# Gate rows by way of memory instead of products of a diagonal with ones

## The chip, the core and the metric

The kernel runs as one program on one core of a Trainium2 chip. The metric is the device time of one execution in microseconds (us). Three executions of the kernel before took 3296.44, 3298.0 and 3299.87 us, median 3298.0.

## The reference

256 tokens of width 2048 pass two blocks, all in float32. The first block is a feed-forward layer, an attention layer and a second feed-forward layer, closed by a norm. The second block has two layers. In each of them, with `c_act = silu(c)` for the token stream and `cc_act = silu(c_ctx)` for a context stream of another 256 tokens:

```python
shift, scale, gate = jnp.split(c_act @ w_mod + b_mod, 3, axis=-1)
shift_c, scale_c, gate_c = jnp.split(cc_act @ w_mod + b_mod, 3, axis=-1)
h = rms_norm(x, norm_g) * (1 + scale) + shift          # the same with _c for the context
p = h @ w_in
x_new = x + gate * mix_out(p, ...)                     # mix_out ends in  @ w_out
xc    = xc + gate_c * mix_out(pc, ...)                 # only in the first of the two layers
```

`gate` and `gate_c` are one row of 2048 numbers each, the same for all tokens. The change is about how this row comes to stand on all 128 partitions, where the residual's sum needs it.

## The kernel before, in words

Tokens lie on partitions in tiles of 128, features on the free axis. The first layer of the second block works on four such tiles (two of tokens, two of context, `nt` = 4), the second layer on two. Every weight matrix is streamed once from memory in units of 512 KB into a ring of four (`raw`), each unit holding two pieces of 128 rows by 512 columns. ScalarE rounds a piece to `hi` (L421), VectorE makes the rest `lo` (L425), and TensorE multiplies each token tile three times per piece: L430 and L431 with `hi`, L435 with `lo`. `hi` and `lo` are rings of four pieces. A piece so takes 6 products with two tiles and 12 with four.

SyncE issues the weight loads (L572), each as soon as the slot's last piece has been made into `lo`. The matrix of the modulation (`wmt`, which gives shift, scale and gate) comes between them: its products are sums on VectorE (L1240, L1242) during the two feed-forward layers of the first block. GpSimd's queue carries other loads: half of `wmt`, small tables, pieces of the norm's gain (`ogc`, L2554) and the context (`cst`, L2564), and writes of x to memory (`x_rest`, L2598, L2614).

The gate lies after `modulation` as `mG[p, layer, stream, k]`, with feature `128 k + p` on partition p (L1192). The out-projection of a layer (`phase o2`) needs it as `gatb[any partition, stream, feature]`. Its 2048 output columns come in four chunks `c` of 512, each with 16 pieces `j`; after chunk c, `add_gated(c, t)` on VectorE multiplies the accumulated tile t by `gatb` (L1887) and adds x (L1892). The gate rows for it are made in strips of 512, eight in the first layer, four in the second, at pieces named in `gate_at`: VectorE lays the gate's numbers on the diagonals of four 128 x 128 blocks (`dg`, L1902), TensorE multiplies a matrix of ones by them (L2520), which puts every number on all partitions, and ScalarE copies the result out of PSUM (L1117).

Each engine runs its own instruction list in order; the places in them are written out by hand as (chunk, piece) positions. `gatb` lies over the last quarter of `qkvg`, which is read for the out-projection's inputs up to the twelfth of its 16 row groups (`o_hi`, `o_low`, L1874).

Of the kernel before, what the change touches and what calls it, by code (L numbers as in the profile page):

```python
# [17 lines left out]
F32 = mybir.dt.float32  # L18
F32R = mybir.dt.float32r
ACT = mybir.ActivationFunctionType  # L20
ALU = mybir.AluOpType
# [77 lines left out]
        self.pieces, self.taken, self.groups, self.fulls, self.turns = pieces, taken, groups, fulls, turns  # L99


def build(nc, a, out, xs_dram):
    ctx = ExitStack()
    with ctx:
        sem_names = """raw0 raw1 raw2 raw3 hi_made lo_made pieces_used acc_done acc_taken tp_done tg_full tg_hi
# [2 lines left out]
            o_done o_taken lam_e ob_made x4_in xs_out ctx_in c_raw c_again modg0 modg1 modd0 modd1 mod_done silu_c  # L108
            ca_const_in glu_made gates_made yt_done yt_taken pl_done pl_taken py_done py_taken pad_made
            conv_step cf_in cf_done z_made cz_done s_made pw_done yc_made na_in bias_in nil_made rot_made  # L110
            st_dve pt_done pt_taken gs_done gs_taken x4r_in fin_in y_out gate_diag rs_made cf_sd zt_done zt_taken w_made og_in s_diag sbc_done mods_made y1_made sig_made ag_made gc_made hq_made tq_done tq_taken
            tmp_made y_made gr_made gt_done gt_taken""".split()
        S = {n: ctx.enter_context(nc.semaphore(n)) for n in sem_names}
        base = (nc.sbuf_base + 63) // 64 * 64
# [59 lines left out]
        cv = at("cv", Q + 73 * K1, [P, 4, 2 * L])  # L174
        ya = at("ya", Q + 83 * K1, [P, 4, CH])
        gC = at("gC", Q + 91 * K1, [P, 4, CH])
        dg = at("dg", Q + 83 * K1, [P, 2, CH])


        Tq = [at("Tq0", H + 4 * K1, [P, CH]), at("Tq1", H, [P, CH])]  # L180
# [161 lines left out]
        def wait(eng, name, value):  # L342

            if not isinstance(value, int) or value > 0:
                eng.wait_ge(S[name], value)
# [8 lines left out]
        def kt_of(n):  # L354

            u, half = spot(n)
            return 2 * u + half

        def gate_at(nt, c, j):

            at_ = ((0, 8), (0, 9), (1, 3), (1, 4), (1, 7), (1, 8), (2, 3), (2, 4)) if nt == 4 else \
                ((0, 8), (1, 3), (2, 3), (3, 3))
            return [at_.index((c, j))] if (c, j) in at_ else []

        def strip_of(nt, i):

            return (i % 2, i // 2) if nt == 4 else (0, i)

        def o_bank(nt, k):

# [294 lines left out]
        def _(act):  # L665
# [330 lines left out]
            for ly in range(2):  # L996
# [114 lines left out]
                def o2_side(c, j, ly=ly, nt=nt):  # L1111
                    if c == 0 and j < 16:
                        o_hi(j)
                    for i in gate_at(nt, c, j - 6):
                        who, k = strip_of(nt, i)
                        act.wait_ge(S["gs_done"], 8 * ly + i + 1)
                        act.activation(gatb[:, who, k * CH:(k + 1) * CH], cg[i % 2][:], ACT.Copy).then_inc(S["gs_taken"], 1)  # L1117
                    if c == 0:
                        return
                    for t in range(nt):  # L1120
                        if j == 5 + 2 * (t // 2) + t % 2:
                            act.wait_ge(S["acc_taken"], phases[f"o2{ly}"].taken + nt * (c - 1) + t + 1)
                            square(sqj2[:, t % 2], x4[:, t, (c - 1) * CH:c * CH], ssp[:, t, c - 1:c])
                    if ly == 0 and j == 10:
                        z_take(zst2, 1, 0, c - 1)
                    if ly == 0 and j == 12:
                        z_take(zst2, 1, 1, c - 1)
                    if c == 3 and j == 14:

                        act.activation(zs[:, 5:6], ones[:, 0:1], ACT.Sqrt)  # L1130
                    if ly == 0 and c == 3 and j == 15:
                        last_sums(ly, nt)
                        z_take(zst2, 1, 0, 3)
# [19 lines left out]
        def _(dve):  # L1153
# [524 lines left out]
            for ly in range(2):  # L1678
# [200 lines left out]
                def add_gated(i, t, ly=ly, nt=nt):  # L1879
                    cols = bass.ds(i * CH, CH)  # L1880
                    if t == 0:
                        if i == 0:
                            dve.wait_ge(S["x4r_in"], 32 if ly == 0 else 48)
                        dve.wait_ge(S["gs_taken"], 8 * ly + nt // 2 * (i + 1))

                    dve.wait_ge(S["acc_taken"], phases[f"o2{ly}"].taken + t - 1 + nt * i)
                    dve.tensor_tensor(tm2[:, t % 2], acc[first_bank(nt, i) + t][:], gatb[:, t // 2, cols], ALU.mult)\  # L1887
                       .then_inc(S["tmp_made"], 1)
                    v = (16 if ly else 0) + t + 1 + nt * i
                    dve.wait_ge(S["tmp_made"], v)  # L1890
                    xv = x4[:, t, cols]
                    dve.tensor_tensor(xv, tm2[:, t % 2], xv, ALU.add).then_inc(S["acc_taken"], 1)  # L1892
                def o2_side(c, j, ly=ly, nt=nt):
                    if c == 0 and j < 16:
                        o_low(j)
                    for i in gate_at(nt, c, j):
                        who, k = strip_of(nt, i)
                        wait(dve, "gs_done", 8 * ly + i - 1)
                        if i == 0:

                            dve.wait_ge(S["tp_done"], phases[f"mx{ly}"].turns + 4)
                        dve.tensor_tensor(dg[:, i % 2].rearrange("p (k n) -> p k n", n=P),  # L1902
                                          ident[:].unsqueeze(1).broadcast_to([P, 4, P]),
                                          mG[:, ly, who, 4 * k:4 * k + 4].unsqueeze(2).broadcast_to([P, 4, P]),
                                          ALU.mult).then_inc(S["gate_diag"], 1)
                    if ly == 0:
                        if c == 0 and j in (6, 9):
                            modulation(1, (6, 9).index(j))
                        if c == 3 and j == 15:
                            for t in range(2):  # L1910
                                bank_done(dve, phases["o20"], 4, 3, t)
                                add_gated(3, t)
                            z_sums(0, 2, 14)
                            dve.tensor_scalar(zv[:, 0:2], zv[:, 0:2], 1.0 / D, EPS, ALU.mult, ALU.add)\
                               .then_inc(S["var_made"], 1)
                            z_reciprocal(0, 2)
                            z_diag(0, 2)
                            bank_done(dve, phases["o20"], 4, 3, 2)
                            add_gated(3, 2)
                    elif c and j in (9, 10):  # L1920
                        dve.wait_ge(S["fin_in"], 16)
                        w_tile(x4, fgain[:, (c - 1) * CH:c * CH], j - 9, c - 1)
# [25 lines left out]
        def _(pe):  # L1948
# [366 lines left out]
            for ly in range(2):  # L2315
# [198 lines left out]
                def o2_side(c, j, ly=ly, nt=nt, ring=ring, o_turn=o_turn):  # L2514
                    if c == 0 and j + ring in O_TURNED:
                        o_turn(j + ring)
                    for i in gate_at(nt, c, j - 1):
                        pe.wait_ge(S["gate_diag"], 8 * ly + i + 1)
                        wait(pe, "gs_taken", 8 * ly + i - 1)
                        pe.matmul(cg[i % 2][:], ones[:], dg[:, i % 2], start=True, stop=True).then_inc(S["gs_done"], 1)  # L2520
                    if ly == 0 and c and j in (8, 10):
                        t0 = j - 8
                        pe.wait_ge(S["acc_taken"], phases["o20"].taken + 4 * (c - 1) + t0 + 2)
                        z_turn(x4, t0, (c - 1) * CH)
# [16 lines left out]
                                 (lambda j, ly=ly: pe.wait_ge(S["tg_lo"], phases[f"mx{ly}"].groups + j + 1))  # L2541
                                 if c == 0 else None, c == 3, x_ready if c == 3 else None)
                if ly == 0:
                    pe.wait_ge(S["gs_taken"], 8)
                    rows_over(2, 0, 2)
                    fill(cg[1], 4)

# [2 lines left out]
        def _(pool):  # L2550
# [38 lines left out]
            for c in range(1, 4):  # L2589
                ctx_load(c)  # L2590
                gain_load(c)
            for ly in range(2):
                nt = NT[ly]

                if ly == 0:
                    for t in range(2):
                        pool.wait_ge(S["x4_in"], t + 1)
                        pool.dma_start(xs_v[:, t], x4[:, t, :]).then_inc(S["xs_out"], 16)  # L2598

                if ly == 1:  # L2600
                    pool.wait_ge(S["conv_step"], 132)

                    pool.wait_ge(S["tg_full"], phases["n41"].fulls + 16 + 6)
                pool.memset(yT[:, :, :, 0:PAD], 0.0).then_inc(S["pad_made"], 1)
                pool.memset(yT[:, :, :, PAD + L:YW], 0.0).then_inc(S["pad_made"], 1)


                pool.wait_ge(S["cf_in"], 32 * (ly + 1))
                pool.memset(nil, 0.0).then_inc(S["nil_made"], 1)
                if ly == 0:  # L2610
                    for c in range(4):

                        pool.wait_ge(S["acc_taken"], phases["o20"].taken + 4 * c + 2)
                        pool.dma_start(xs_v[:, :, c * CH:(c + 1) * CH], x4[:, 0:2, c * CH:(c + 1) * CH])\  # L2614
                            .then_inc(S["xs_out"], 16)
            pool.wait_ge(S["tg_lo"], phases["o21"].groups)
            pool.dma_start(fgain[:], row_bc(a["final_norm_g_2"], D)).then_inc(S["fin_in"], 16)

# [25 lines left out]
```

## Time and profile before

| | us |
|---|---|
| median of three executions | 3298.0 |
| lowest, highest | 3296.44, 3299.87 |
| span of the profiled execution (first to last instruction) | 3296.4 |
| TensorE busy in it | 3250.2 |
| VectorE busy | 2271.8 |
| ScalarE busy | 1554.2 |
| GpSimd busy | 90.8 |

The profile gives the profiled execution's own time as this span alone; the three times are of other executions, and their median lies 1.6 us above it. "Busy" counts overlapping instructions once. A matmul's duration in the profile is the time from its start to its modelled end; since matmuls are pipelined, what one costs is the distance between starts.

### The profile page before, as it was taken

Reading aid. Unit: us, or ns where it says so; the run is one execution under the profiler, and the core shown is the slowest. Engines: PE = TensorE matmul, PEld = TensorE weight load, DVE = VectorE, ACT = ScalarE, POOL = GpSimd, SP = SyncE. Lnnn points to the kernel's source line nnn. Section 1 sums busy time; section 2 is a strip of 40 time slices with the busy share of each in tenths; the row PEclk is TensorE's granted clock in tenths of the full one; section 3 lists DMA queues with packets and bytes.
Section 4 is the critical chain, followed back from the end, with each engine's and each line's share of the span. In section 5 each row is a group of like instructions: output and inputs, shape, how many; then the busy total and the mean of one; then the engine's idle time right before and its main releaser. Section 6 shows DMA issues by size and latency. Waiting matters only on the chain.

```text
span 3296.4 us, 40653 instructions
## 1 busy us (share of the span) xinstructions
PE 3250.2 (99%) x15142; PEld 2650.1 (80%) x15142; DVE 2271.8 (69%) x4132; ACT 1554.2 (47%) x2872; POOL 90.8 (3%) x174
## 2 busy tenths in 40 slices
PE   9999999999999999999999999999999999999998
PEld 7888888888888788888888788888866778888766
DVE  7888888877776788888877633557556437746666
ACT  6545454445665555445555422222256336522464
POOL 0000000000000000000000000000000000000000
PEclk9999999999999999999999999999999999999999
DMA  8888877776545888788877432333322236533525
GB/s 285 261 267 262 258 260 259 251 260 197 153 147 173 260 260 268 260 259 260 268 261 264 131 104 89 95 100 96 96 80 78 86 100 192 181 116 96 176 72 171
DMA packets 285316, 614.21 MB, mean 186 GB/s; under 512 B 18688, under 2 KB 21312, under 8 KB 283456
## 3 DMA queue, kind: packets, MB, share of 16 engines
q1 hardware_dynamic: 261792, 527.50, 50.0%
q0 software_dynamic: 21952, 80.69, 7.5%
q10 hardware_dynamic: 1376, 3.44, 0.3%
q8 instruction: 120, 1.97, 0.2%
q14 instruction: 76, 0.62, 0.1%
HBM read 605.26 MB, written 6.29 MB: 186 GB/s over the span
## 4 chain that ended last, share of the span: by engine, by line
PE 93%; ACT 2%; DVE 2%; DMA 1%; issue 1%; SPq 0%; ACTq 0%; DVEq 0%
PE acc L430 29%; PE acc L431 28%; PE acc L435 28%; PE tp L2434 1%; PE acc L2455 1%; PE acc L2420 1%; DMA raw<-ffn_w_gu 1%; PE tp L2393 1%; PE tp L2002 1%; ACT pr L1068 0%; PE cgw L2405 0%; DVE lo L425 0%; PE cgw L2155 0%; PE tp L1964 0%; ACT hi L421 0%
## 5 line engine op out<-in xcount | busy, mean ns | idle before, releaser
L421 ACT ACTIVATE hi<-raw 128x512 fp32r<-128x512 f32 x1808 | 1135.1, 632 | 1546.7 <-PE acc L435 1472.5
L425 DVE TENSOR_TENSOR lo<-raw,hi 128x512 fp32r<-128x512 f32 x1808 | 1208.3, 689 | 832.4 <-ACT hi L421 823.3
L430 PE MATMUL acc<-hi,hT_hi 128*128 128x512 f32 x1760 | 696.2, 396 | 9.3 <-DVE hT_lo L1227 4.9
L431 PE MATMUL acc<-hi,hT_lo 128*128 128x512 f32 x1760 | 685.4, 389 | 0.0
L430 PE MATMUL acc<-hi,h_hi 128*128 128x512 f32 x1696 | 670.9, 396 | 6.8 <-ACT hi L421 3.8
L431 PE MATMUL acc<-hi,h_lo 128*128 128x512 f32 x1696 | 662.0, 390 | 0.0
L435 PE MATMUL acc<-lo,h_hi 128*128 128x512 f32 x1696 | 533.9, 390 | 0.4 <-DVE lo L425 0.4
L435 PE MATMUL acc<-lo,hT_hi 128*128 128x512 f32 x1760 | 513.6, 389 | 0.0
L430 PEld LDWEIGHTS acc<-hi,hT_hi 128*128 128x128 f32 x1760 | 330.4, 188 | 87.9 <-DVE hT_lo L1227 8.9
L431 PEld LDWEIGHTS acc<-hi,hT_lo 128*128 128x128 f32 x1760 | 330.6, 188 | 69.1 <-issue 2.6
L435 PEld LDWEIGHTS acc<-lo,hT_hi 128*128 128x128 f32 x1760 | 330.5, 188 | 69.1
L430 PEld LDWEIGHTS acc<-hi,h_hi 128*128 128x128 f32 x1696 | 319.1, 188 | 74.4 <-ACT hi L421 5.5
L435 PEld LDWEIGHTS acc<-lo,h_hi 128*128 128x128 f32 x1696 | 319.2, 188 | 68.6 <-DVE lo L425 0.8
L431 PEld LDWEIGHTS acc<-hi,h_lo 128*128 128x128 f32 x1696 | 319.4, 188 | 64.5
L430 PE MATMUL acc<-hi,uT_hi 128*128 128x512 f32 x704 | 275.3, 391 | 0.5 <-DVE lo L425 0.5
L431 PE MATMUL acc<-hi,uT_lo 128*128 128x512 f32 x704 | 274.0, 389 | 0.0
L1240 DVE CUSTOM_DVE_ANT_0 cgw<-mw,cb 128x1024 f32<-128x1024 f32 x192 | 235.6, 1227 | 0.7 <-DMA mw<-wmt 0.7
L1242 DVE CUSTOM_DVE_ANT_0 mw<-mw,cb 128x1024 f32<-128x1024 f32 x192 | 234.5, 1221 | 0.0
L435 PE MATMUL acc<-lo,uT_hi 128*128 128x512 f32 x704 | 219.9, 389 | 0.0
L1742 DVE SCALAR_TENSOR_TENSOR cv<-yT,dw,cv 128x512 f32<-128x512 f32 (+1 forms) x256 | 156.7, 612 | 0.0
L430 PEld LDWEIGHTS acc<-hi,uT_hi 128*128 128x128 f32 x704 | 132.2, 188 | 28.3 <-DVE lo L425 1.4
L435 PEld LDWEIGHTS acc<-lo,uT_hi 128*128 128x128 f32 x704 | 132.2, 188 | 27.7
(283 smaller groups left out, 2155.9 us busy)
## 6 DMA issues: line engine op xcount, KB each, us to landing
raw<-ffn_w_gu SPq DMA_DIRECT2D x352, 512.0 KB, 5.8
raw<-w_in SPq DMA_DIRECT2D x280, 512.0 KB, 3.8
raw<-ffn_w_down SPq DMA_DIRECT2D x176, 512.0 KB, 5.4
mw<-wmt POOLq DMA_DIRECT2D x132, 512.0 KB, 5.6
raw<-w_out SPq DMA_DIRECT2D x96, 512.0 KB, 4.1
mw<-wmt SPq DMA_DIRECT2D x60, 512.0 KB, 5.9
ball<-rpbx SPq DMA_DIRECT2D x8, 768.0 KB, 9.8
x<-x_rest SPq DMA_DIRECT2D x2, 2048.0 KB, 7.8
```

What stands on the lines that cost most here:

```text
L421: act.activation(hi[:, g % RING, :], raw_piece(g), ACT.Copy).then_inc(S["hi_made"], 1)
L425: dve.tensor_tensor(lo[:, g % RING, :], raw_piece(g), hi[:, g % RING, :].bitcast(F32), ALU.subtract).then_inc(S["lo_made"], 1)
L430: pe.matmul(bank, act_hi, hi[:, slot, :], start=start, stop=False)
L431: pe.matmul(bank, act_lo, hi[:, slot, :], start=False, stop=False)
L435: return pe.matmul(bank, act_hi, lo[:, slot, :], start=False, stop=stop)
L1240: dve.tensor_tensor_reduce(cgw[:].rearrange("p a n -> p (a n)"), w, c[:, 0], 1.0, 0.0, ALU.mult, ALU.add, dst[:, 0:1])
L1242: dve.tensor_tensor_reduce(w, w, c[:, 1], 1.0, 0.0, ALU.mult, ALU.add, dst[:, 1:2])\
L1742: dve.scalar_tensor_tensor(out=av, in0=yv, scalar=dw[:, ly, bass.ds(j * 16 + s, 1)], in1=av, op0=ALU.mult, op1=ALU.add).then_inc(S["conv_s ...
L2002: ins = pe.transpose(tp[f][:, k * L + t * P:k * L + (t + 1) * P], ub[:, t, (2 * f + k) * P:(2 * f + k + 1) * P], ident[:])
L2393: ins = pe.matmul(tp[t % 2][:], sT[:, t % 2, c * P:(c + 1) * P], cpw[:, c, :], start=(c == 0), stop=(c == 3))
L2420: ins = pe.matmul(acc[e][:], q[r, t * P:(t + 1) * P], kk[r, :], start=True, stop=True)
L2434: ins = pe.transpose(tp[u % 2][:, j * P:(j + 1) * P], src, ident[:])
```

## The change

The twelve strips made with diagonals, products with ones and copies go away, with their buffer and semaphores. Instead GpSimd's queue writes both gate rows of a layer to a small buffer in memory (`gate_rows`, 2 layers x 2 streams x 2048), and in the out-projection reads each chunk's 512 columns back with a partition step of zero, so that all 128 partitions get the same row. The write of the first layer stands behind the loads of `ogc` and `cst`, that of the second behind the writes of `x_rest` in the first layer's out-projection. The reads stand in each layer behind the `memset` of `nil`, and wait for the write and for the twelfth row group. `add_gated` waits for its chunk's read.

```diff
-def build(nc, a, out, xs_dram):
+def build(nc, a, out, xs_dram, gate_rows):
-        dg = at("dg", Q + 83 * K1, [P, 2, CH])
@@ ScalarE, out-projection
-                    for i in gate_at(nt, c, j - 6):
-                        who, k = strip_of(nt, i)
-                        act.wait_ge(S["gs_done"], 8 * ly + i + 1)
-                        act.activation(gatb[:, who, k * CH:(k + 1) * CH], cg[i % 2][:], ACT.Copy).then_inc(S["gs_taken"], 1)
@@ VectorE, add_gated
-                        dve.wait_ge(S["gs_taken"], 8 * ly + nt // 2 * (i + 1))
+                        dve.wait_ge(S[f"gat_in{i}"], 16 * (ly + 1))
@@ VectorE, out-projection
-                    for i in gate_at(nt, c, j):
-                        who, k = strip_of(nt, i)
-                        wait(dve, "gs_done", 8 * ly + i - 1)
-                        if i == 0:
-                            dve.wait_ge(S["tp_done"], phases[f"mx{ly}"].turns + 4)
-                        dve.tensor_tensor(dg[:, i % 2]..., ident..., mG[:, ly, who, 4 * k:4 * k + 4]..., ALU.mult)
@@ TensorE, out-projection
-                    for i in gate_at(nt, c, j - 1):
-                        pe.wait_ge(S["gate_diag"], 8 * ly + i + 1)
-                        wait(pe, "gs_taken", 8 * ly + i - 1)
-                        pe.matmul(cg[i % 2][:], ones[:], dg[:, i % 2], start=True, stop=True).then_inc(S["gs_done"], 1)
...
-                    pe.wait_ge(S["gs_taken"], 8)
@@ GpSimd
+            def gates_out(ly):
+                pool.wait_ge(S["mods_made"], 2 * ly + 2)
+                pool.dma_start(gate_rows[ly].rearrange("w (k p) -> p w k", p=P), mG[:, ly], allow_slow_non_contiguous=True).then_inc(S["gm_out"], 16)
+
+            gates_out(0)
             for ly in range(2):
...
                 pool.memset(nil, 0.0).then_inc(S["nil_made"], 1)
+                pool.wait_ge(S["gm_out"], 16 * (ly + 1))
+                pool.wait_ge(S["tg_lo"], phases[f"mx{ly}"].groups + 12)
+                for c in range(4):
+                    rows = bass.AP(tensor=gate_rows.tensor, offset=gate_rows[ly, 0, c * CH:(c + 1) * CH].offset,
+                                   ap=[[0, P], [D, nt // 2], [1, CH]])
+                    pool.dma_start(gatb[:, 0:nt // 2, c * CH:(c + 1) * CH], rows).then_inc(S[f"gat_in{c}"], 16)
                 if ly == 0:
...
+                    gates_out(1)
```

## Rows read from the trace of the kernel before

**Rows 1.** The page's first part: engine, busy us, share, instructions.

```profile
PE 3250.2 (99%) x15142; PEld 2650.1 (80%) x15142; DVE 2271.8 (69%) x4132; ACT 1554.2 (47%) x2872; POOL 90.8 (3%) x174
```

**Rows 2.** The chain that ended last, shares, 2530 to 2745 us.

```profile
by line: PE acc L430 27.7%; PE acc L431 26.8%; PE acc L435 26.8%; PE cgw L2520 3.2%; DVE tm L1887 2.9%; PE tp L1964 2.6%; issue 2.5%; PE tp L2508 1.5%; DVE x L1892 1.1%; PE acc L2455 0.8%; PE cgw L1952 0.8%; ACT hi L421 0.7%; ACT zst L727 0
```

**Rows 3.** The same chain, shares, 3180 us to the end.

```profile
by line: PE acc L430 24.4%; PE acc L431 23.9%; PE acc L435 23.9%; PE cgw L2520 2.9%; PE acc L2455 2.6%; PE acc L2420 1.9%; PE tp L2434 1.8%; ACT x L1146 1.7%; ACT pr L1063 1.3%; issue 1.2%; ACT hi L421 1.0%; PE tp L2508 0.7%; ACT L1130 0.6%
```

**Rows 4.** Timeline of TensorE: start us, us, engine, line, what.

```profile
2559.88 1.07 PE L435 MATMUL acc<-lo,hT_hi 128*128 128x512 f32 x4
2562.60 1.07 PE L435 MATMUL acc<-lo,hT_hi 128*128 128x512 f32 x4
2563.51 1.02 PE L2520 MATMUL cgw<-dg,ones 128*128 128x512 f32 x2
2566.19 1.07 PE L435 MATMUL acc<-lo,hT_hi 128*128 128x512 f32 x4
```

**Rows 5.** By tile: duration ns min/median/max, first and last start us.

```profile
L2520 PE MATMUL cgw<-dg,ones x24: 590/591/595, 2563.5 to 3268.7; 128*128 128x512 f32 x24
...
L1902 DVE TENSOR_TENSOR dg<-ident,mG x12: 683/686/692, 2552.0 to 3264.9; 128x512 f32<-128x512 f32 x12
...
L1117 ACT ACTIVATE gatb<-cgw x12: 579/580/622, 2575.5 to 3271.3; 128x512 f32<-128x512 f32 x12
```

**Rows 6.** The page's groups: busy us, mean ns, idle before.

```profile
L421 ACT ACTIVATE hi<-raw 128x512 fp32r<-128x512 f32 x1808 | 1135.1, 632 | 1546.7 <-PE acc L435 1472.5
L425 DVE TENSOR_TENSOR lo<-raw,hi 128x512 fp32r<-128x512 f32 x1808 | 1208.3, 689 | 832.4 <-ACT hi L421 823.3
```

**Rows 7.** Timeline of GpSimd around the two new writes.

```profile
1771.83 0.58 POOL L2554 DMA_DIRECT2D ogc<-out_norm  x1 [34.10 <-DVE x L1583]
1843.86 0.56 POOL L2598 DMA_DIRECT2D x_rest<-x  x1 [71.45 <-ACT x L976]
...
2726.90 0.72 POOL L2614 DMA_DIRECT2D x_rest<-x  x1 [42.18 <-DVE x L1892]
```

**Rows 8.** DMA queues, 744 to 762 us: packets, MB, share of 16 engines.

```profile
q1 hardware_dynamic: 1434, 2.78, 46.7%
q0 software_dynamic: 464, 0.98, 34.0%
```

**Rows 9.** DMA queues, 750 to 755 us.

```profile
q0 software_dynamic: 254, 0.48, 75.8%
q1 hardware_dynamic: 226, 0.42, 22.9%
```

**Rows 10.** Landing of weight loads (L572) issued in 744 to 764, then 1740 to 1810 us.

```profile
DMA to landing us min/median/max: 3.7/5.1/10.2
...
DMA to landing us min/median/max: 3.9/5.4/9.1
```

**Rows 11.** Waits of ScalarE: us, times, longest; 740 to 775, then 1770 to 1790 us.

```profile
ACT hi L421 <- DMA raw<-w_in: 2.6, 1, 2.6
...
ACT hi L421 <- DMA raw<-ffn_w_down: 1.9, 1, 1.9
```

**Rows 12.** Windows: us, busy PE, PEld, DVE, ACT, POOL; PEclk, DMA share, GB/s.

```profile
1760.00:1780.00 20.00, 20.00 (x90) 16.57 (x89) 16.38 (x28) 11.94 (x23) 0.58 (x1) 1.00 0.76 243
...
2724.00:2734.00 10.00, 9.96 (x49) 8.13 (x48) 6.46 (x14) 5.57 (x14) 0.72 (x1) 1.00 0.22 82
...
3210.00:3215.00 5.00, 5.00 (x25) 4.11 (x24) 3.12 (x6) 2.69 (x6) 0.55 (x1) 1.00 0.59 170
```

**Rows 13.** Timeline of VectorE: twelfth row group in each layer, first use in the second.

```profile
2559.54 0.68 DVE L1874 TENSOR_TENSOR hT_lo<-qkvg,hT_hi 128x512 fp32r<-128x512 f32 x1
...
3205.81 0.42 DVE L1874 TENSOR_TENSOR hT_lo<-qkvg,hT_hi 128x256 fp32r<-128x256 f32 x1
...
3215.74 0.69 DVE L1887 TENSOR_TENSOR tm<-acc,gatb 128x512 f32<-128x512 f32 x1 [0.62 <-PE acc L435]
```

**Rows 14.** First layer's uses of the gate rows, first and last start.

```profile
L1887 DVE TENSOR_TENSOR tm<-acc,gatb x15: 682/684/692, 2581.7 to 2728.6; 128x512 f32<-128x512 f32 x15
```

**Rows 15.** DMA issues: size of each, median us from issue to landing.

```profile
ogc<-out_norm POOLq DMA_DIRECT2D x4, 256.0 KB, 5.9
psc<-pool_scale SPq DMA_DIRECT2D x2, 256.0 KB, 7.7
```

More of the change, by code:

```diff
@@ L110, in build @@
             conv_step cf_in cf_done z_made cz_done s_made pw_done yc_made na_in bias_in nil_made rot_made
-            st_dve pt_done pt_taken gs_done gs_taken x4r_in fin_in y_out gate_diag rs_made cf_sd zt_done zt_taken w_made og_in s_diag sbc_done mods_made y1_made sig_made ag_made gc_made hq_made tq_done tq_taken
+            st_dve pt_done pt_taken gm_out gat_in0 gat_in1 gat_in2 gat_in3 x4r_in fin_in y_out rs_made cf_sd zt_done zt_taken w_made og_in s_diag sbc_done mods_made y1_made sig_made ag_made gc_made hq_made tq_done tq_taken
             tmp_made y_made gr_made gt_done gt_taken""".split()
@@ L357, in kt_of @@
             return 2 * u + half
[L359 to L367, printed above, removed]
         def o_bank(nt, k):
@@ L1895, in o2_side @@
                         o_low(j)
-                    for i in gate_at(nt, c, j):
-                        who, k = strip_of(nt, i)
-                        wait(dve, "gs_done", 8 * ly + i - 1)
-                        if i == 0:
-                            dve.wait_ge(S["tp_done"], phases[f"mx{ly}"].turns + 4)
[L1902 to L1905, printed above, removed]
                     if ly == 0:
@@ L2640 @@
     xs = nc.dram_tensor("x_rest", (L, D), F32, kind="Internal").ap()
-    build(nc, aps, out, xs)
+    gates = nc.dram_tensor("gate_rows", (2, 2, D), F32, kind="Internal").ap()
+    build(nc, aps, out, xs, gates)
     r = run_bass_kernel_spmd(nc, [arrays], core_ids=[0])
```

## The prediction

> **What bounds the kernel now.** I read the page's busy shares first: TensorE is busy 3250.2 of 3296.4 us [rows 1], so a microsecond that TensorE need not spend is worth nearly a microsecond wherever nothing else ends later. Then the chain of waits of the two stretches in which the gate rows are made and used: of the first layer's out-projection (2530 to 2745 us) 3.2% is L2520, the products with ones [rows 2]; of the stretch from 3180 us to the end it is 2.9% [rows 3]. The diagonals (L1902) and the copies (L1117) don't appear in either list. So TensorE's part of the old way is on the path and the other two parts are beside it. Third, because the change puts new transfers on GpSimd's queue, the timeline of that queue, the share of the DMA engines in windows, and how late weights land.
>
> **What goes from TensorE.** The timeline shows the price of one strip: L435 starts at 2559.88, 2562.60 and 2566.19 [rows 4]. A piece without a strip takes 2.72 us, the one with it 3.59, so a strip costs 0.87 us. Each is recorded as two passes of 591 ns, 24 records for 12 strips [rows 5]; their distance counts, not their sum. 12 x 0.87 is 10.4 us. The chain gives the same by another way: 3.2% of 215 us is 6.9, 2.9% of 116.4 us is 3.4, together 10.3 [rows 2, 3]. I take 10.3.
>
> **What goes from VectorE and ScalarE.** 12 x 0.686 = 8.2 us and 12 x 0.580 = 7.0 us [rows 5]. Both lie beside TensorE's products; ScalarE spends most of its idle time waiting for TensorE [rows 6]. I put 0 for them. If TensorE then met something later, it would be VectorE's row groups in the first chunk, and these get earlier too.
>
> **The new write of gate rows, first layer.** It is issued right behind the load of `ogc`, at 1772.4 us; GpSimd's next instruction in the old order comes at 1843.86 [rows 7], so 71 us of delay in the queue would hide. The issue itself took 0.56 to 0.72 us in neighbouring DMAs [rows 7]. Its result is needed some 790 us later. What it can cost is the weights: by the change's own access pattern a partition's neighbouring numbers lie 512 bytes apart in memory, so this is 2 x 16 x 128 = 4096 pieces of 4 bytes, 256 for each DMA engine, while the last feed-forward projection streams its weights.
>
> The trace has nothing of 4 bytes. The nearest are GpSimd's 13 small loads of tables at 744 to 752 us: from the tile shapes, 2176 rows of 128 to 1024 bytes, with 13 x 16 = 208 completions 2384 items. They took 34.0% of 16 engines over 18 us, 97.9 us of engine time for 0.98 MB; the weights beside them took 134.5 us for 2.78 MB, 48.4 us per MB [rows 8]. So an item cost 41 ns in all, or 21 ns when the bytes are taken out at the weights' rate. A far upper end is the densest window's 60.6 us for 254 packets, 239 ns, if each 4-byte piece cost as much as such a packet [rows 9]. For one engine's 257 items (256 and a completion) that is 5.4, 10.5 or 61 us. I take 31 ns, between the two lower values, since the pieces carry no bytes to speak of but go to memory: 8.0 us.
>
> While they drain, the weights' queue is pushed back: in the densest window it had 22.9% of the engines beside 75.8% for GpSimd's [rows 9], where the stretch at 1760 to 1780 us uses 0.76 [rows 12]. Weights are then late by 1 - 0.229/0.76 = 0.70 of the drain: 3.8, 5.6, 7.4 or 43 us.
>
> How much lateness is free? A weight load in this stretch lands 5.4 us after its issue in the median, 9.1 at the most, and ScalarE waited 1.9 us for one [rows 10, 11]. Taking these as the same load, `hi` is wanted 7.2 us after the issue. With four `hi` pieces in the ring and 1.36 us per piece (half of 2.72, two tiles instead of four), a `hi` that starts on time stands three pieces, 4.1 us, before TensorE needs it, less 0.63 and 0.69 us for making `hi` and `lo` [rows 6]: 2.8 us more. So 10.0 us from issue to TensorE, of which 5.4 are used: 4.6 us are free. The small loads at 744 us agree: a load landed at 10.2 instead of 5.1 us, ScalarE waited 2.6 us [rows 10, 11]. The stall is 5.6 - 4.6 = 1.0 us; at 21 ns 0, at 41 ns 2.8, at 239 ns 38.
>
> The Trainium skill says in "DMA: Bandwidth & Descriptors", section "Rules for kernel authors", that a non-contiguous last dimension becomes one descriptor per element, and in its "Queues, rings and completion order" that an engine changes between queues only at packet boundaries, a packet holding up to 64 descriptors. The trace agrees that small descriptors push the weights back (22.9% [rows 9]); by the rule with 64 pieces to a packet the weights would get even less than I assume, and complete exclusion at 41 ns would make the stall 10.5 - 4.6 = 5.9 us instead of 2.8. No row here shows packets of 4-byte pieces.
>
> **The write of the second layer** comes behind the last `x_rest` at 2726.90 [rows 7]. There the engines are used to 0.22 [rows 12] and with four tiles a piece lasts 2.72 us, so twice the lateness is free. 0 us; with the 61 us drain it would reach into the next layer and cost some 10.
>
> **The reads back.** First layer: GpSimd waits until the twelfth row group, 2559.54 + 0.68 = 2560.2 us, then issues four reads of 512 KB. The first use is at 2581.7 [rows 13, 14], 21 us later, or some 20 when two strips are gone. Second layer: released at 3206.2, first use at 3215.74 [rows 13], less one strip 3214.9: 8.7 us for a broadcast of 256 KB. The same kind of load from the same queue (`ogc`) landed in 5.9 us, `psc`, which stood behind others, in 7.7 [rows 15]. Both fit, by 2.8 and 1.0 us. The later chunks have 21 us and more. The 1 MB read there fits beside weights that use 0.59 of the engines [rows 12]; 0 us, up to 2 if a weight unit is held back. Behind the new wait in `add_gated` stand the `lo` pieces of the next chunk on VectorE, and TensorE waits for them; behind GpSimd's new waits stand only the `x_rest` writes of the first layer, wanted after the first chunk, and `fgain`, wanted 20 us later.
>
> **The sum.** -10.3 + 1.0 = -9.3 us. Against the profiled span, 3296.4 to 3287.1; the median stands 1.6 us above that span, so 3288.7, rounded 3289.
>
> **The rivals.**
> 1. The 4-byte write eats most of the gain: its items cost 48 to 81 ns, the stall is 0.70 x 257 x price - 4.6 = 4 to 10 us. For it: writes to memory in pieces this small are outside all rows; against it: 21 to 41 ns in rows 8. At 60 ns: stall 6.2, time 3294.
> 2. Slower: the same write starves the weights for good. Break-even is a stall of 10.3, at 83 ns; measurably slower from 119 ns. At 150 ns the drain is 38.6 us, late by 27, stall 22.4: 3310. For it: the 239 ns packet in rows 9; against it: that packet carried 1.9 KB.
> 3. The reads in the second layer come late: at 12 us instead of 5.9 VectorE waits 3.3 us, its slack of under 1 us is gone, and TensorE loses about 3: 3292. For it: only 1.0 us of cover by `psc`.
> 4. TensorE's freed time is refilled by a wait: 3298. Against it: L1902 and L1117 are on neither chain [rows 2, 3].
>
> **How the numbers follow.** What a measurement of this kernel can tell from no change is about 0.2%, 6.6 us. Forecast 0.55 (all of it faster by over 6.6), rival 1 0.21, rival 3 0.05 and rival 4 0.03 (all within), rival 2 0.16 (slower). So 0.55, 0.29, 0.16. The likeliest case's own range is 3287.7 (no stall) to 3290.5 (2.8 us of it) and 1 us around it for the medians. The range for all reaches through rival 1 and into rival 2: 3286 to 3302.
>
> **What would show it.** Right: no L2520, L1902, L1117; pieces of 2.72 us throughout the out-projection; GpSimd with two small DMAs near 1772 and 2727 us and eight reads; DMA share near 1.0 for some 8 us after 1772 and at most one wait of `hi` for weights there with under 2 us of TensorE idle; VectorE's first L1887 in each layer still released by TensorE. Wrong: a wait of TensorE of over 4 us between 1772 and 1830 us, `tm` waiting for the gate read, or the landing of the small write beyond 20 us.

## Result and the profile after

The changed kernel takes 3304.45 us (median of 13 executions, 3299.67 to 3308.91) beside 3298.15 us for the kernel before (13 executions, 3296.32 to 3300.53): ratio 1.0019, 95% interval 1.0011 to 1.0026. It is slower by some 6 us, where 9 us less was forecast, and the time lies outside the range that was given (3286 to 3302 us). The profiled execution took 3306.85 us with a span of 3305.0.

The page's first part shows that the products are gone: 24 TensorE instructions fewer than in [rows 1], 12 fewer each on VectorE and ScalarE, ten more on GpSimd.

```profile
PE 3245.9 (98%) x15118; PEld 2648.1 (80%) x15118; DVE 2264.0 (69%) x4120; ACT 1547.6 (47%) x2860; POOL 99.2 (3%) x184
```

TensorE's busy time fell by only 4.3 us though 10.3 us of products left, and the span grew by 8.6. GpSimd's timeline tells where time came in. It is to be laid beside [rows 7]:

```profile
1772.25 0.58 POOL L2524 DMA_DIRECT2D ogc<-out_norm  x1 [34.10 <-DVE x L1568]
1772.82 1.70 POOL L2565 DMA_DIRECT2D gate_rows<-mG  x1
1859.59 0.57 POOL L2574 DMA_DIRECT2D x_rest<-x  x1 [85.06 <-ACT x L965]
...
2734.05 0.72 POOL L2596 DMA_DIRECT2D x_rest<-x  x1 [42.21 <-DVE x L1877]
2734.76 1.71 POOL L2565 DMA_DIRECT2D gate_rows<-mG  x1
2799.03 0.21 POOL L2580 MEMSET yT<- 128x120 f32 x1 [62.56 <-DVE tm L1204]
```

Up to the first new write the two kernels run within 0.5 us of each other. The next landmark stood at 1843.86 us and stands at 1859.59: 15.7 us lost, or 15.3 when both are counted from the `ogc` load just before the write. The last `x_rest` write of the first layer's out-projection stood at 2726.90 and stands at 2734.05, so by then 8.6 us have been won back; the eight strips of this layer explain 7.0 of it (8 x 0.87). The next landmark, the filling of `yT`, was at 2788.02 us in the profile before and is at 2799.03: 11.0 us late, so 3.9 us were lost behind the second write. The four strips of the second layer bring the difference to 8.6 us at the end.

The chain of waits names the carrier at both places; columns are start, us, what:

```profile
1778.18 23.30 DMA raw<-ffn_w_down
...
2741.93 12.36 DMA raw<-w_in
```

A weight load issued at 1778.18 us, 5.4 us behind the small write, took 23.3 us instead of the 5.4 of [rows 10]. The one before it, issued at 1776.84 us, took 20.9. TensorE's waits around the first and the second write (columns as in [rows 11]):

```profile
PE acc L419 <- ACT hi L410: 10.7, 2, 9.9
...
PE acc L419 <- ACT hi L410: 2.7, 1, 2.7
```

And the windows over the first, columns as in [rows 12]; the first line is of the kernel before, the others of the change:

```profile
1778.00:1790.00 12.00, 12.00 (x59) 10.03 (x58) 7.70 (x13) 7.45 (x17) 0.00 (x0) 1.00 0.83 267
...
1778.00:1790.00 12.00, 10.53 (x51) 8.48 (x49) 5.12 (x9) 3.99 (x8) 0.00 (x0) 1.00 1.13 64
1790.00:1798.00 8.00, 0.00 (x0) 0.00 (x0) 0.00 (x0) 0.21 (x1) 0.00 (x0) 0.56 0.92 114
1798.00:1808.00 10.00, 8.75 (x20) 6.39 (x21) 6.17 (x10) 4.76 (x11) 0.00 (x0) 0.50 0.74 274
```

Two things are to be seen. The DMA engines are recorded as fully busy while they move 64 GB/s, where the same stretch before moved 267. (The view adds up the times of packets, which overlap, so the share can pass 1.) And after TensorE has stood idle, it works at half its clock: the granted clock is 0.50, that is 1.2 instead of 2.4 GHz, from about 1791 to 1808 us, and TensorE works in it from 1798.5 on. The starts of its products lie 0.43 us apart there instead of 0.23. So the loss of 15.3 to 15.7 us is 10.7 us of waiting and some 4.5 us of slow products after it.

The queues from 1783 to 1793 us, columns as in [rows 8]:

```profile
q1 hardware_dynamic: 299, 0.68, 98.4%
q0 software_dynamic: 19, 0.00, 5.4%
```

The small write hardly shows as a user of the engines. It is the weights' own packets that got long: 98.4% of 16 engines over 10 us for 299 packets, 527 ns each. In the kernel before the same 10 us held 1335 packets of this queue with 82.7%, 99 ns each.

The reads back did what was expected. Landing of the four reads of the first layer and of the second, and VectorE's first use in the second layer:

```profile
DMA to landing us min/median/max: 7.8/9.6/10.1
...
DMA to landing us min/median/max: 6.0/6.7/7.7
...
3226.57 0.69 DVE L1872 TENSOR_TENSOR tm<-acc,gatb 128x512 f32<-128x512 f32 x1 [0.62 <-PE acc L424]
```

The second layer's reads were issued from 3218.2 us and landed within 7.7 us, before 3226.57, and the use still waited for TensorE, not for the read. The cover was 0.7 us (8.4 us from issue to use).

### The profile page after: what moved, and what is told of

It reads as the page before. It is cut to its first block, busy times and chain, and to the rows that moved or that the text cites. A ratio compares the mean times of both kernels' runs of the same rounds, so it can differ in the third digit from the quotient of the medians.

```text
span 3305.0 us, 40581 instructions
## 1 busy us (share of the span) xinstructions
PE 3245.9 (98%) x15118; PEld 2648.1 (80%) x15118; DVE 2264.0 (69%) x4120; ACT 1547.6 (47%) x2860; POOL 99.2 (3%) x184
## 4 chain that ended last, share of the span: by engine, by line
PE 93%; ACT 2%; DVE 2%; DMA 2%; issue 1%; SPq 0%; ACTq 0%; DVEq 0%
PE acc L419 29%; PE acc L420 28%; PE acc L424 28%; PE tp L2409 1%; PE acc L2430 1%; PE acc L2395 1%; DMA raw<-ffn_w_down 1%; PE tp L2368 1%; PE tp L1977 1%; DMA raw<-ffn_w_gu 1%; ACT pr L1057 0%; PE cgw L2380 0%; DVE lo L414 0%; PE cgw L2130 0%; DMA raw<-w_in 0%
## 5 line engine op out<-in xcount | busy, mean ns | idle before, releaser
L419 PE MATMUL acc<-hi,uT_hi 128*128 128x512 f32 x704 | 277.3, 394 | 11.2 <-ACT hi L410 10.7
```

Source lines behind the costliest of these rows:

```text
L419: pe.matmul(bank, act_hi, hi[:, slot, :], start=start, stop=False)
```

## Experiments

Theory after the trace: the whole loss comes from the writes of the gate rows, 4096 pieces of 4 bytes each, which hold up weight loads; the rest of the change is worth its 10.3 us of gain. Rivals: the reads or the new waits cost too; the cost is fixed per DMA; it comes from GpSimd's descriptor making; it comes from the number of pieces at the DMA engines; it comes from writing 4 bytes to memory. All ratios are against the kernel before on the same chip. In every kernel below `second_late`, and in `second_late` itself, the second layer's write goes in the attention stage as in `late`; where the first place has only a copy (`contig`, `onchip`, `spread`, `own_rows`), the first layer's real write goes there too.

| kernel | median us | ratio | 95% interval | against `late`, us | first write in the trace, us |
|---|---|---|---|---|---|
| the change | 3304.45 | 1.0019 | 1.0011 to 1.0026 | +16 | +15.3 |
| late | 3288.79 | 0.9970 | 0.9958 to 0.9981 | | +0.1 |
| writes_only | 3317.29 | 1.0055 | 1.0042 to 1.0069 | | +9.8 |
| second_late | 3299.12 | 1.0001 | 0.9992 to 1.0010 | +10 | +9.2 |
| half | 3295.14 | 0.9986 | 0.9977 to 0.9996 | +5 | +5.6 |
| contig | 3288.96 | 0.9969 | 0.9957 to 0.9981 | 0 | +0.1 |
| onchip | 3289.34 | 0.9963 | 0.9952 to 0.9975 | -2 | 0.0 |
| actq | 3301.12 | 1.0007 | 0.9998 to 1.0017 | +12 | +11.3 |
| paced | 3316.16 | 1.0054 | 1.0036 to 1.0071 | +28 | +29.0 |
| parted | 3296.39 | 0.9992 | 0.9982 to 1.0002 | +7 | +7.2 |
| spread | 3293.91 | 0.9980 | 0.9971 to 0.9990 | +3 | +5.2 |
| own_rows | 3306.48 | 1.0023 | 1.0014 to 1.0032 | +17 | +18.4 |

The fifth column is the difference of the ratios times 3298. Both ratios have their intervals, and `late` was measured on one chip only, so this column is good to some 5 us. The last column is taken within one execution: the distance from the `ogc` load to the next `x_rest` write [rows 7], less the 72.0 us that it has in the kernel before. Where nothing is lost it repeats within 0.2 us (before, `late`, `contig`, `onchip`). The three traces with the same whole write from GpSimd's queue (the change, `writes_only`, `second_late`) differ by 6 us among themselves.

**late**: both writes at a quiet time.

```diff
-            gates_out(0)
...
                 pool.memset(nil, 0.0).then_inc(S["nil_made"], 1)
+                pool.wait_ge(S["bias_in"], 64 * (ly + 1))
+                gates_out(ly)
                 pool.wait_ge(S["gm_out"], 16 * (ly + 1))
...
-                    gates_out(1)
```

> Both writes of the gate rows moved to each layer's attention, after the bias has landed, when the DMA engines are nearly idle. Theory (the whole loss is the two writes colliding with the weight loads at 1772 and 2735 us): the 10.3 us of the products remain, 3298.2 - 10.3 = 3287.9, within 2 us; no wait of ScalarE for weights over 3 us anywhere, clock 0.997. Rival (the reads back, or the new waits, cost as well): 3291 or more. Rival (the products' time is refilled): 3296 or more.

Measured 3288.79 us, as the theory had it. Its other sign did not hold as stated: ScalarE still has a wait of 5.0 us for weights, in the first block; the kernel before has one of 4.8 there. The write sits at 2430.8 and 3122.4 us, 130 and 79 us ahead of the reads. The stretch from 1770 to 1810 runs at full clock. TensorE's timeline at the place of the first strip, to be read beside [rows 4]:

```profile
2562.78 1.07 PE L424 MATMUL acc<-lo,hT_hi 128*128 128x512 f32 x4
2565.50 1.07 PE L424 MATMUL acc<-lo,hT_hi 128*128 128x512 f32 x4
```

2.72 us between them where the strip had made it 3.59. This version beats both kernels, by 10 and 16 us. What the reads, the waits and the order of the change cost is too small to be measured (the interval of `late` is 4 us to either side).

**writes_only**: the kernel before, and only the two `gates_out` added at the change's places, with a wait for them before the load of `fgain`.

> The kernel before with the two writes of the gate rows added at the places of the change; the rows are not read, the strips are made as before. Theory: plus 15 to 20 us (profile of the change: 15.8 at the first write, 3.9 at the second), 3313 to 3318. Rival (the collision needs something else of the change): under 3305.

3317.29 us, 18 us above the kernel before. So the writes need nothing else of the change to do their harm, and -10.3 + 18.4 gives the change's result to 2 us.

**second_late**: the first write where the change has it, the second moved as in `late`.

> The first write where the change has it, the second in the second layer's attention. Theory: the second write costs 3.9 us, so 3304.5 - 3.9 = about 3300.5. Rival (the second write only moves a wait that other work would have hidden): 3304.

3299.12 us: of the 16 us that lie between the change and `late`, the first write makes 10 and the second about 6 by the ratios. The trace of the change had 15.7 and 3.9 in one execution; the single executions of such kernels scatter (3296.44 to 3304.63 here). The one in this trace was the shortest: TensorE waited 6.4 us for `hi`, and the first write cost 9.2.

**half**: at the first place only stream 0, 2048 pieces; stream 1 goes in the attention stage. `gates_part(ly, w, k0, k1)` writes columns `k0` to `k1` of stream `w`.

```diff
-            gates_out(0)
...
+            gates_part(0, 0, 0, KT)
```

> At the first place only the token stream's row is written, 2048 pieces instead of 4096; the context's row and the second layer's rows go in the attention stages. Theory by pieces (lateness of a weight load grows with their number, 17.9 us for 4096, and 4.6 us are free): lateness 9, stall 4.4 us, TensorE's clock does not fall, 3287.9 + 4.4 = 3292. Rival (a fixed cost per such write): about 3300, like with the whole one. Rival (threshold): 3288.

3295.14 us, +5 where +4.4 was expected and +10 is the whole write; in its trace +5.6. So about half the pieces, half the cost: no threshold that 2048 stay under, and no fixed cost of the size of the whole. The intervals alone would not tell `half` from `late`, but `late` has no wait of TensorE for `hi` at this place and `half` has one of 3.8 us. That TensorE's clock would not fall was wrong: the granted clock of 1780 to 1790 us was 0.83. The proportion is then partly chance, since the free slack should have taken more of the half than of the whole.

**contig**: the same 16 KB as 128 rows of 128 bytes at the first place.

```diff
+            pool.wait_ge(S["mods_made"], 2)
+            pool.dma_start(gate_copy[:], mG[:, 0].rearrange("p w k -> p (w k)")).then_inc(S["gm_out"], 16)
```

> At the first place the same 16 KB go to memory as 128 rows of 128 bytes (a copy nobody reads); the rows that are read are written in the attention stages as in the run late. Theory (the number of 4-byte pieces makes the delay): no stall, 3289, like late. Rival (any write from GpSimd's queue there delays the weights): over 3293.

3288.96 us, nothing lost. A write to memory at that place is free when it is 128 pieces of 128 bytes.

**onchip**: 4096 pieces of 4 bytes, 8 bytes apart in each partition, but into a tile on chip whose contents nobody needs then.

```diff
+            pool.wait_ge(S["mods_made"], 2)
+            for w in range(2):
+                pool.dma_start(qss[:].rearrange("p a b -> p (a b)")[:, 0:2 * KT].rearrange("p (k w) -> p w k", w=2)[:, :, w],
+                               mG[:, 0, w], allow_slow_non_contiguous=True).then_inc(S["gm_out"], 16)
```

> At the first place 4096 pieces of 4 bytes go, in two DMAs of 2048, from the gate's tile to another tile on chip (nobody reads it) instead of to memory; the rows that are read are written in the attention stages. Theory A (the engines' work per piece delays the weights): 3299, like second_late. Theory B (4-byte writes to memory are what is slow): 3289, like late.

3289.34 us, nothing lost: theory B. As many pieces, the same queue, and no harm. GpSimd's issue of each DMA took 1.16 us, as long as the issue of 2048 pieces in `half` (1.17), so as much was made of it. Its DMAs of 2048 pieces landed in 7.9 and 8.3 us, where the 2048 of `half`, to memory and beside the same weights, took 14.5. The number of pieces alone does not hold up the weights; that they go to memory does. The Trainium skill says in "DMA: Bandwidth & Descriptors", section "Why small descriptors are slow (HBM only)", that transfers within SBUF don't suffer the penalty of small descriptors; the run agrees (+0 on chip, +10 to memory).

**actq**: the first write at the same time from ScalarE's hardware queue.

```diff
+                if c == 3 and j == 13:
+                    act.wait_ge(S["mods_made"], 2)
+                    act.dma_start(gate_rows[0].rearrange("w (k p) -> p w k", p=P), mG[:, 0],
+                                  allow_slow_non_contiguous=True).then_inc(S["gm_act"], 16)
```

> The first write at the same time and of the same 4096 pieces, but issued by ScalarE into its hardware queue; the second write in the attention stage. If the delay comes from GpSimd's making of descriptors: 3289, like late. If it comes from the pieces at the DMA engines or in memory: about 3299, like second_late, or more if the issue holds ScalarE up.

3301.12 us, +12, no less than `second_late` within the intervals: GpSimd's queue is not the cause. Here the pieces are recorded one by one. The queues from 1773 to 1793 us:

```profile
q1 hardware_dynamic: 923, 2.05, 68.4%
q10 hardware_dynamic: 4082, 0.02, 55.8%
```

4082 packets took 55.8% of 16 engines over 20 us, 178.6 us, 43.7 ns each. The write landed after 24.4 us.

**paced**: the first write in eight parts (one stream, four of its 16 columns `k` each), one every three pieces of the weights' stream (`gates_out(0)` goes away here and in `parted`, as in `half`).

```diff
+            for n in range(8):
+                pool.wait_ge(S["pieces_used"], phases["d2"].pieces + 3 * DK + 12 + 3 * n)
+                gates_part(0, n // 4, 4 * (n % 4), 4 * (n % 4) + 4)
```

> The first write in eight parts of 512 pieces, one every three pieces of the weights' stream (4.1 us) from the middle of the same chunk of the feed-forward projection; the second write in the attention stage. Theory (a burst makes a weight load late by some 4.4 us per 1024 pieces and only what exceeds 4.6 us stalls): each part delays by 2.2 us, 3289 to 3291. Rival (every piece costs, whenever it comes): 3299.

3316.16 us, +28: my theory and its rival were both far off. Splitting made it almost three times as bad. Landing of the eight parts:

```profile
DMA to landing us min/median/max: 10.0/13.0/15.8
```

A part with an eighth of the pieces took 13.0 us in the median, where the whole write takes 14.0 to 14.6 with almost nothing beside it (`late`) and 16.4 to 21.7 beside weights (the change). A part's pieces all go to four stretches of 512 bytes, 128 pieces of 4 bytes to each, one from every partition. That suggested theory L: what takes the time is the many small writes into the same stretch of memory.

**parted**: eight parts at the same times, but of 16 partitions each.

```diff
+                rows = slice(16 * n, 16 * n + 16)
+                pool.dma_start(gate_rows[0].rearrange("w (k p) -> p w k", p=P)[rows], mG[rows, 0],
+                               allow_slow_non_contiguous=True).then_inc(S["gm_out"], 16)
```

> The real first write in eight parts at the same times as in paced, 512 pieces each, but split by partitions: a part brings 16 neighbouring pieces to each of the 32 stretches of 512 bytes, where a part of paced brings all 128 to each of four. The second write is in the attention stage. Theory L: a part's time goes with the pieces per stretch, 16 instead of 128, so each lands in under 6 us instead of 10 to 16 and the weights hardly wait: 3289 to 3293. Theory M: 3316, like paced.

3296.39 us, +7 instead of +28, and the parts landed sooner:

```profile
DMA to landing us min/median/max: 5.0/7.3/8.7
```

Same pieces, same pace, same final addresses; what differs is which pieces travel together. A part of `paced` brings 128 to each of four stretches, from all 128 partitions; one of `parted` brings 16 to each of 32, from 16 partitions. That the grouping decides is shown: 20 us lie between the two. Whether it is the number per stretch or the number of source partitions is not, since both change at once. And the cost is not gone as theory L hoped: 3296 instead of 3289 to 3293, landings up to 8.7 us instead of under 6.

**spread** and **own_rows**: 4096 pieces in one DMA at the first place, to other addresses.

```diff
+            pool.dma_start(gate_copy[:, :, 0], mG[:, 0].rearrange("p w k -> p (w k)"),
+                           allow_slow_non_contiguous=True).then_inc(S["gm_out"], 16)
...
+    copy = nc.dram_tensor("gate_copy", (P, 2 * KT, 128), F32, kind="Internal").ap()
```

This is `spread`; `own_rows` has 2 in place of 128.

> At the first place 4096 pieces of 4 bytes go to memory in a copy nobody reads, each to a stretch of 512 bytes of its own; the rows that are read are written in the attention stages. Theory L (what is slow is that 128 partitions, so 16 engines, write 4 bytes each into the same 512 bytes): no or little stall, 3289 to 3291. Theory M (every 4-byte write to memory is slow, whatever its address): 3299, like second_late.

> As in spread, but each partition's 32 pieces go to 256 bytes of their own, 8 bytes apart, so that only pieces of one partition are neighbours. Theory L (writes of different engines into the same stretch): 3289 to 3291. Theory M (every small write to memory): 3299. Between the two if neighbours of one engine also disturb each other.

`spread` is 3293.91 us, between the two theories. The ratios give +3, which their intervals would not tell from nothing, its trace +5.2: TensorE waited 2.8 us for `hi` there, and not at all at this place in the kernel before, `late`, `contig` and `onchip`. So a piece that is alone in its 512 bytes costs less than in the real write, and not nothing. `own_rows` is 3306.48, +17, worse than the real write and outside both theories; it landed after 26.4 us. Its pieces lie 8 bytes apart, as those of `onchip` do, which cost nothing.

So theory L in its narrow form (writes of different engines into one stretch) falls: the 32 pieces of one partition, 8 bytes apart, are worse than 128 pieces of 128 partitions, 4 bytes apart. Nor is it simply the number per stretch: 512 bytes of `own_rows` get 64 pieces and those of the real write 128. What is left is that 4-byte pieces with near neighbours cost more than lone ones (+10 and +17 against +3), and that it matters which pieces go together (`paced` against `parted`). No run separates the rest: whether the neighbours of one engine or their order in time count most, and whether the weights wait because the DMA engines are held by their own unfinished writes or because memory itself is slow. The Trainium skill's "Specifications" in "DMA: Bandwidth & Descriptors" says that below 512 bytes a transfer is done as read-modify-write; a chain of such steps on one stretch would fit, but no run here shows the step itself.

## Why the prediction was wrong

**Held.** A strip's 0.87 us and the sum of 10.3: `late` has 10.2 us less than its kernel before. VectorE's and ScalarE's 8 and 7 us hidden: `late` again. The reads back hidden, in the second layer with little to spare: landed in at most 7.7 us of the 8.4 there were (8.7 forecast). The issue hidden in GpSimd's queue: 1.70 us instead of 0.56 to 0.72, beside 71.

**The step that failed** is the drain of the 4-byte write, taken as 8.0 us (257 items of 31 ns per engine) in bounds of 5.4 to 10.5 us that I held for good and a far end of 61. In engine time an item costs 43.7 ns (`actq`), 11.2 us per engine, just above the upper of the near bounds. But the time in which the weights were held back was far longer: the write alone needs 14.0 to 14.6 us to land (`late`), beside the weights 21.7 us, the longer of the change's two:

```profile
DMA to landing us min/median/max: 14.0/14.3/14.6
...
DMA to landing us min/median/max: 16.4/19.0/21.7
```

The first of these lines is of `late`, the second of the change. My rows for an item's price were loads into the chip [rows 8, 9], where nothing is written to memory in small pieces. For a target on chip the price was about right: in `onchip` all 4096 pieces had landed some 9.4 us after the first issue, at most 37 ns per item. The 22.9% that I read as small descriptors pushing the weights back [rows 9] is of packets that carried 1.9 KB, no less than the weights' own, and says nothing of 4-byte pieces. I had named "writes to memory in pieces this small are outside all rows" as a reason for rival 1 and still placed the value between two numbers of the wrong kind.

**The share of the weights**, 0.30 of their need while the write drains, was near: 0.68 MB in the 10 us from 1783 are 68 GB/s, 0.28 of the 243 in [rows 12], and from 1779 to 1796 us the weights moved 0.84 MB where they moved 4.21 before, 0.20. But it held because the weights' packets grew to 527 ns, not because the small packets took the engines.

**The free slack** of 4.6 us was 1 us too small. The load that ended the long wait took 20.9 us, was late by 15.5, and TensorE waited 9.9: 5.6 were free.

**The stall with the right drain.** A drain of 21.7 us is 84 ns per item, and the prediction's form makes 0.70 x 21.7 - 4.6 = 10.6 us of stall of it, where 10.7 were measured. That this fits so well is partly luck: the loads were late by 15.5 and 17.9 us and not by 15.2, and the slack was larger too. So the form of the stall was sound, and its input was wrong by a factor of 2.7.

**Left out**: TensorE's clock. In the change's trace the wait of 9.9 us was followed by some 9 us of work at half clock, which cost some 4.5 us more. After the 6.4 us of `second_late` the granted clock was 0.66 from 1790 to 1800 us; after the 2.7 us at the second write it stayed at 1.00. No term of the sum had this, and neither had rival 2.

**The second write**, put at 0 because of twice the slack, cost 3.9 us in the trace and 5.3 in the medians (the change against `second_late`). It was issued at 2734.76, in the last pieces of the out-projection; weight loads of the next stage, which runs with two tiles and half the slack, were caught: the load of 2741.93 took 12.4 us.

Two of the signs that had been named for a wrong forecast came: a wait of TensorE of over 4 us between 1772 and 1830 us (9.9), and a landing of the small write beyond 20 us (21.7). The third did not: `tm` never waited for a gate read.

The mechanism that came true is that of rivals 1 and 2, the 4-byte write. By the measured price it was neither quite: 84 ns lies at rival 2's break-even of 83, above which it was held at 0.16, and the gain was then overtaken by the clock and by the second write, which no rival had priced. The 6.3 us that the change lost lie just under the 6.6 that the prediction wanted before it spoke of slower, so by its own classes the outcome was the one held at 0.29.

## What to carry to other kernels

A DMA that scatters 4-byte pieces into memory is not priced by its bytes, nor by its pieces: here it made the weight loads beside it take up to four times as long until it had landed. Put it where nothing streams (here the attention stage, where it cost nothing), or turn the layout on chip first so that whole rows are written (not tried; `contig` shows that 128 whole rows cost nothing there). Cutting it in parts is no remedy: it made things almost three times as bad when each part took a few columns of all partitions, and gained some 3 us (+7 against +10) when each took all columns of a few partitions. When a stream has a slack of a few microseconds, ask of any new transfer how long it may take to land, and add the slow clock that can follow a stall of TensorE.

## What had not been expected of the hardware

- 4096 pieces of 4 bytes held back the weights by 10 us of kernel time when written to memory, and by nothing when written on chip (3299.12 and 3289.34 us).
- The place in memory matters: +3 us (+5 in the trace) with each piece in 512 bytes of its own, +10 for 4-byte neighbours of different partitions, +17 for a partition's own pieces 8 bytes apart.
- Eight DMAs of 512 pieces cost +28 us when each brings 128 pieces to four stretches of 512 bytes, and +7 when each brings 16 pieces to 32 stretches.
- GpSimd's queue records such a write as few packets and a small share (5.4% from 1783 to 1793 us), ScalarE's as 4082 packets with 55.8% of the engines, for the same effect: the share of a queue does not tell what it does to the others.
